# Ranking a router's experts: half-size lists packed two products to a matmul, and the fullest expert read once

## The reference, cut to what matters

```python
def moe_swiglu(x, w_router, w1, w3, w2):      # 8 experts, top 2, hidden width 3584
    ...
    logits = (xf @ w_router).astype(jnp.float32)
    top_vals, top_idx = lax.top_k(logits, TOP_K)
    gates = jax.nn.softmax(top_vals, axis=-1)
    ...
        return (jax.nn.silu(xb @ w1[e]) * (xb @ w3[e])) @ w2[e]
    ...
    out = jax.ops.segment_sum(y, tok_buf, num_segments=n)
...
        e = jax.nn.sigmoid(h @ ple_gate_w[i] + ple_gate_b[i]) * (p[i] @ ple_w[i])
        h = layer_norm(DEEPNORM_ALPHA * h + f + e, ln2_g[i], ln2_b[i])
```

## Time and profile before

| | us |
|---|---|
| device time, median of 3 runs | 2062.16 |
| lowest and highest | 2061.69, 2062.79 |
| the profiled execution: span from first to last instruction | 2060.3 |
| PE busy in that span | 2035.3 |
| DVE, ACT busy | 1579.0, 1269.3 |

### The profile page before, as it was taken

One profiled execution on the slowest core, in us unless ns is written; L12 is line 12 of the kernel. 1 busy time (PEld: TensorE's weight loads), 2 busy tenths in 40 slices (PEclk: granted clock), 3 DMA queues, 4 the chain that ended last, 5 costly groups with the idle time before them and its releaser, 6 DMA issues.

```text
span 2060.3 us, 29349 instructions
## 1 busy us (share of the span) xinstructions
PE 2035.3 (99%) x10989; PEld 1699.0 (82%) x10989; DVE 1579.0 (77%) x1430; ACT 1269.3 (62%) x1272; POOL 163.2 (8%) x134
## 2 busy tenths in 40 slices
PE   9999999999999999999999999999999999999998
PEld 8977897778889998987778888888888888888876
DVE  7767544687666557679988888888888888888897
ACT  7666433453644334466677777777777777777674
POOL 0031010000214000021400000000000000000100
PEclk9999999999999999999999999999999999999999
DMA  6533594237555555726999999999999999999995
GB/s 254 186 103 105 196 358 169 83 131 261 159 185 202 189 185 187 255 90 228 358 412 383 367 384 370 371 380 368 382 370 381 368 371 380 368 382 370 383 381 211
DMA packets 88065, 580.41 MB, mean 282 GB/s; under 512 B 10144, under 2 KB 13472, under 8 KB 22064
## 3 DMA queue, kind: packets, MB, share of 16 engines
q1 hardware_dynamic: 79472, 548.26, 70.7%
q0 software_dynamic: 7904, 29.95, 4.0%
q10 hardware_dynamic: 608, 1.07, 0.2%
HBM read 559.96 MB, written 15.73 MB: 279 GB/s over the span
## 4 chain that ended last, share of the span: by engine, by line
PE 91%; DVE 4%; DMA 1%; issue 1%; ACT 1%; POOL 0%; DVEq 0%; ACTq 0%; SPq 0%
PE bank L642 84%; PE bank L1414 1%; DMA ring<-in_w_moe 1%; DVE wrest L2634 1%; PE bank L857 1%; PE bank L1217 1%; DVE wrest L2040 0%; DMA cst<-in_consts 0%; PE bank L860 0%; PE bank L1385 0%; PE bank L1031 0%; PE bank L945 0%; PE bank L975 0%; PE bank L1224 0%; ACT ohi L1737 0%
## 5 line engine op out<-in xcount | busy, mean ns | idle before, releaser
L2634 DVE TENSOR_TENSOR wrest<-ring,whi 128x2048 fp32r<-128x2048 f32 x378 | 853.7, 2304 | 77.7 <-ACT whi L1939 77.3
L1939 ACT ACTIVATE whi<-ring 128x2048 fp32r<-128x2048 f32 x374 | 699.2, 1918 | 84.1 <-DMA ring<-in_w_moe 82.0
L642 PE MATMUL bank<-whi,xgT 128*128 128x512 f32 x1008 | 404.7, 402 | 3.0 <-DVE wrest L2634 3.0
L642 PE MATMUL bank<-wrest,xgT 128*128 128x512 f32 x1008 | 396.3, 393 | 0.0
L642 PE MATMUL bank<-whi,xgR 128*128 128x512 f32 x1008 | 393.5, 390 | 0.0
L642 PEld LDWEIGHTS bank<-whi,xgT 128*128 128x128 f32 x1008 | 189.5, 188 | 47.3 <-DVE wrest L2634 7.1
L642 PEld LDWEIGHTS bank<-whi,xgR 128*128 128x128 f32 x1008 | 189.5, 188 | 46.6
L642 PEld LDWEIGHTS bank<-wrest,xgT 128*128 128x128 f32 x1008 | 188.9, 187 | 38.7
L642 PE MATMUL bank<-whi,hidE 128*128 128x512 f32 x504 | 201.8, 400 | 0.8 <-DVE wrest L2634 0.8
L642 PE MATMUL bank<-wrest,hidE 128*128 128x512 f32 x504 | 197.8, 392 | 0.0
L642 PE MATMUL bank<-whi,hidR 128*128 128x512 f32 x504 | 196.8, 390 | 0.0
(11 more groups left out here) (483 smaller groups left out, 3688.5 us busy)
## 6 DMA issues: line engine op xcount, KB each, us to landing
ring<-in_w_moe SPq DMA_DIRECT2D x378, 1024.0 KB, 4.9
ring<-in_w_dense SPq DMA_DIRECT2D x135, 1024.0 KB, 4.8
row<-in_rows POOLq DMA_DIRECT2D x17, 512.0 KB, 5.2
xg_rows<-ncR POOLq DMA_DIRECT2D x12, 512.0 KB, 25.2
y_rows<-arena POOLq DMA_DIRECT2D x9, 512.0 KB, 6.2
arena<-xg_rows SPq DMA_DIRECT2D x9, 512.0 KB, 5.4
arena<-arena SPq DMA_DIRECT2D x32, 106.5 KB, 3.8
arena<-in_tbias POOLq DMA_DIRECT2D x2, 1536.0 KB, 8.8
```

The lines of the kernel that those rows point to most:

```text
L642: ins = pe.matmul(out_, lhsT, rhs, start=start, stop=stop, **more)
L1939: S["w_hi"].on(a.activation(whi[:, n % HI_SLOTS, :], ring[:, c % RING, :], ACT.Copy))
L2634: S["w_lo"].on(v.tensor_tensor(wrest[:, s, :], ring[:, s, :], whi[:, n % HI_SLOTS, :].bitcast(F32), ALU.subtract))
```

## The change

The experts are ranked by their counts (`rank_of`). Three kinds of list take the place of one.

- **Mid lists.** Ranks 1 and 2 (`MIDS` = 2), and one extra list for each expert that holds more than its cap, run as loops through `mid_list`, which is the old list code. The caps are 192 tokens for rank 0, 128 for ranks 1 and 2, 64 for the rest.
- **Small lists.** Ranks 3 to 7 have at most 64 tokens in them. The rounded part and the rest of the activations lie side by side in one stationary operand of 128 (`packed`), and a chunk costs two matmuls per block in place of three: 8 in all (`pair_product`). The two halves of the result's rows are added by a product with `fold_ones`, which also transposes (`fold`, eight float32 matmuls of 64 columns); ACT copies the w1 and w3 products to SBUF for it (`copy_h1`, `copy_h3`).
- **The big list.** Rank 0's weights are read once for 192 tokens: 128 by `split_product` (12 matmuls a chunk) and 64 more by `pair_product` (8), 20 in all. Its outputs are added in `y_big` by DVE, four 512-column additions a step (`add_big`).

The big list's 42 chunks and the small lists' 210 are merged in one written-out order of 252 places: a big chunk every 5.25 places up to place 215, then 36 small chunks. In this late part there are eight raw places and four rounded ones: two of `whi`'s six places become raw ones. Of the experts' weights none is loaded before the ranks are known, and two gather products stand behind the embedding gate's last chunk.

```diff
+N_SMALL, HALF = 5, P // 2
+LATE_RING, LATE_HI = 8, 4
+MIDS, EXTRAS = 2, 4
+BLOCKS = 1 + MIDS + EXTRAS + (1 + N_SMALL) // 2
...
-EMBED_AT, Y_AT = (4, 8, 12, 15, 18, 21), (20, 24, 28, 32)
+EMBED_AT, Y_AT = (4, 8, 12, 15, 18, 21), (234, 238, 242, 246)
+PAIR_LOADED, PAIR_TURNED, LAST_TURNED = (20, 112), (34, 129), 160
...
+def _merged_order():
+
+    small = []
+    for t in range(SMALL_STEPS):
+        small += [("small", t, c) for c in range(4)]
+        if t:
+            small += [("small", t - 1, c) for c in (4, 5)]
+    small += [("small", SMALL_STEPS - 1, c) for c in (4, 5)]
+    big = [("big", d, c) for d in range(E_STEPS) for c in range(6)]
+    places = {k * 21 // 4 for k in range(len(big))}
+    small, big = iter(small), iter(big)
+    return [next(big) if m in places else next(small) for m in range((1 + N_SMALL) * E_CHUNKS)]
...
+FOLD_AT = [min(m for m in range(AT["small", t, 3] + 1, LAST) if ORDER[m][0] == "small") for t in range(SMALL_STEPS)]
+BIG_FOLD_AT = [AT["big", d, 3] + 2 for d in range(E_STEPS)]
...
-            def expert(i, e):
+            def mid_list(i, e):
...
-            with sp.Fori(0, N_EXP) as e:
-                expert(e, e)
+                sp.dma_start(xg, xg_rows[bass.ds((i + 2) * P, P), :]).then_inc(x_in, 16)
...
             wait(sp, "router_done", 1)
-            n = sp.value_load(plan_i[0:1, 0:1], min_val=N_EXP, max_val=LISTS)
...
+            mid_list(0, expert_id(0))
+            wait(sp, "router_done", 3)
+            mids = sp.value_load(plan_i[0:1, ID_LISTS:ID_LISTS + 1], min_val=MIDS, max_val=MIDS + EXTRAS)
...
+            for m, (kind, step, c) in enumerate(ORDER):
+                if kind == "small" and step % E_STEPS == 0 and c == 0:
+                    small_ids[step // E_STEPS] = expert_id(ID_SMALL + step // E_STEPS)
+                e = big_id if kind == "big" else small_ids[step // E_STEPS]
+                sp.wait_ge(chunks_used.sem, mids * E_CHUNKS + (N_DENSE + (min(m - RING + 1, 0) if m < LATE_RING
+                                                                         else m - LATE_RING + 1)))
+                sp.dma_start(late_raw(m), w_moe[bass.ds(e * E_CHUNKS + in_expert(step % E_STEPS, c), 1)]
+                             .rearrange("a p n -> p (a n)")).then_inc(late_ready(m), 16)
+                if m in PAIR_LOADED:
...
+            def gather_first():
+
+                wait(pe, "places", 1)
+                gather_product(sel, (2, 3), "m_g")
+                wait(pe, "places", 2)
+                wait(pe, "pg_in", 6)
+                gather_product(selg, half_banks[0], "b_g")
...
-                        gather_first()
...
+                if i:
+                    gather_first()
...
+            def fold(bank, parts, done):
+
+                for n in range(2):
+                    for b in range(4):
+                        ins = pe.matmul(ps[bank][:, 256 * n + HALF * b:256 * n + HALF * b + HALF],
+                                        parts[n][:, b * P:(b + 1) * P], fold_ones, start=True, stop=True, skip_group_check=True)
+                S[done].on(ins)
+
...
+            def small_second(m, t, half):
+
+                l, j = divmod(t, E_STEPS)
...
+                wh, wr = late_chunk(m, 4)
+                for k in range(4):
+                    kk = 4 * (c % 2) + k
+                    split_product(ps[4 + c // 2][:, :], (big_x[0][:, kk, :], big_x[1][:, kk, :]),
+                                  (wh[:, k, :], wr[:, k, :]), kk == 0, kk == KT - 1)
...
+                for k in range(4):
+                    kk = 4 * (c % 2) + k
+                    ins = pair_product(ps[6 + c // 2][:, :], packed[:, PACKED_BIG, kk, :], (wh[:, k, :], wr[:, k, :]),
+                                       kk == 0, kk == KT - 1)
+                chunks_used.on(ins)
...
-            round_ahead(0)
-            round_ahead(1)
             wait(a, "r_top", 2)
             S["r_e"].on(a.activation(g12[:, 1, :], g12[:, 0, :], ACT.Exp))
-            round_ahead(2)
             gate_embedding(1, 0)
             round_gathered(0, 2)
+            round_ahead(0)
+            wait(a, "b_g", 1)
+            for n in range(2):
+                S["b_xa"].on(a.activation(big_x[0][:, 4 * n:4 * n + 4, :],
+                                          ps[half_banks[0][n]][:, :].rearrange("p (k n) -> p k n", k=4), ACT.Copy))
+            round_ahead(1)
+            gate_embedding(1, 1)
+            round_ahead(2)
             round_ahead(3)
-            gate_embedding(1, 1)
...
+            def copy_h1(t):
+                finished("small", t, 1)
+                wait(a, "s_fold", t)
+                S["s_copy1"].on(a.activation(s13[0], ps[0][:, :], ACT.Copy))
...
+            for m in range(AHEAD, LAST + 1):
+                wait_late(a, m, mids)
+                a.wait_ge(chunks_used.sem, mids * E_CHUNKS + (N_DENSE + m - LATE_HI + 1))
+                S["w_hi"].on(a.activation(whi[:, m % LATE_HI, :], late_raw(m), ACT.Copy))
+                if m == AHEAD:
+                    copy_outputs(mids)
+                for d in range(E_STEPS):
+                    if m == AT["big", d, 1] + 2:
+                        silu_big(d)
+                        copy_big(d, 0)
+                    if m == AT["big", d, 3] + 2:
+                        copy_big(d, 1)
...
+                for t in range(SMALL_STEPS):
+                    if m == AT["small", t, 1] + 2:
+                        copy_h1(t)
+                    if m == AT["small", t, 3] + 2:
+                        copy_h3(t)
+                    if m == FOLD_AT[t] + 2:
+                        silu_small(t)
+                    if m == min(FOLD_AT[t] + 4, LAST):
+                        round_small(t)
...
+            def add_big(d, n):
+
+                finished("big", d, 5)
+                wait(v, "b_y", 4 * d)
+                for c in range(2):
+                    part, bank = y_big[n][:, 512 * c:512 * c + 512], ps[4 + 2 * n + c][:, :]
+                    S["b_y"].on(v.tensor_tensor(part, part, bank, ALU.add) if d else v.tensor_copy(part, bank))
...
+            for m in range(AHEAD, LAST + 1):
+                wait(v, "w_hi", mids * E_CHUNKS + (MOE_ROUNDED + m + 1))
+                S["w_lo"].on(v.tensor_tensor(late_rest(m), late_raw(m), whi[:, m % LATE_HI, :].bitcast(F32), ALU.subtract))
```

More of the change, by code:

```diff
@@ L597, in _ @@
                         power(rstd[:, j:j + 1], 1)
[L600 removed]
+            wait(pool, "places", 3)
             wait(pool, "ple_done", 20)
@@ L1457, in expert_list @@
                         second(j - 1, j if j == E_STEPS - 1 else None)
-                if not last:
-                    turn_gathered(i)
+                turn_gathered(i)
                 second(E_STEPS - 1)
                 assert n[0] == E_CHUNKS and over[0] == 1
-            with pe.Fori(0, last_list) as i:
-                expert_list(i, False)
-            wait(pe, "places", 3)
-            wait(pe, "pg_in", 8)
-            for t in range(2):
-                ins = pe.transpose(ps[5][:, t * P:(t + 1) * P], selg[:, t, :], ident)
@@ L1469, in _, with late_chunk, pair_product @@
-            S["place_ps"].on(ins)
-            expert_list(last_list, True)
-            wait(pe, "places", 4)
+            with pe.Fori(0, mids) as i:
+                mid_list(i)
+            def late_chunk(m, k):
+                wait(pe, "w_lo", mids * E_CHUNKS + (MOE_RESTS + m + 1))
+                form = "p (k n) -> p k n"
+                return whi[:, m % LATE_HI, :].rearrange(form, k=k), late_rest(m).rearrange(form, k=k)
+            def pair_product(out_, both, w, start, stop):
+                mm(out_, both, w[0], start=start, stop=False, skip_group_check=True)
+                return mm(out_, both, w[1], start=False, stop=stop, skip_group_check=True)
@@ L1473, in _ @@
+            assert over[0] == 0
+            wait(pe, "b_y", 4 * E_STEPS)
             for q in range(4):
@@ new lines, in finished, with copy_h3 @@
+            def finished(kind, step, c):
+                a.wait_ge(chunks_used.sem, mids * E_CHUNKS + (N_DENSE + AT[kind, step, c] + 1))
+            def copy_h1(t):
+                finished("small", t, 1)
+                wait(a, "s_fold", t)
+                S["s_copy1"].on(a.activation(s13[0], ps[0][:, :], ACT.Copy))
+            def copy_h3(t):
+                finished("small", t, 3)
+                wait(a, "s_fold", t)
+                S["s_copy3"].on(a.activation(s13[1], ps[1][:, :], ACT.Copy))
@@ new lines, in silu_small, with round_small, copy_low @@
+            def silu_small(t):
+                wait(a, "s_fold", t + 1)
+                wait(a, "s_hid", t)
+                S["s_sl"].on(a.activation(slT, ps[1][:, 0:SEQ], ACT.Silu))
+            def round_small(t):
+                wait(a, "s_hid", t + 1)
+                if t >= 2:
+                    finished("small", t - 2, 5)
+                S["s_hi"].on(a.activation(hidP[t % 2][:, :, 0:HALF], hidT.rearrange("p (b n) -> p b n", b=4), ACT.Copy))
+            def copy_low(l):
```

(21 more changed lines are left out.)

542 lines of the change are left out of this document (436 added, 106 removed).

## The result

| | before | after |
|---|---|---|
| device time, median of 4 runs | 2062.12 us | 1981.71 us |
| lowest and highest | 2061.69, 2062.79 | 1979.84, 1982.41 |
| span of the profiled execution | 2060.3 us | 1979.3 us |

The ratio is 0.9609, with a 95% interval of 0.9595 to 0.9622: 80 us less, where the prediction had 111 less (1951, range 1895 to 2000). It is past the forecast's own narrower range, 1930 to 1975.

What follows compares the result with a forecast made beforehand. PE was taken as the bound. Mid lists ending at 1213.0 us (start's 12.7 included), late part 721 and end 14.7 gave span 1948.7; with about 1.9 for device time, 1951 us, range 1895 to 2000.

Steps and rivals of the forecast that it cites:

- The sum of the parts: Likeliest case, whole kernel: start, mid lists, late part and end added up to 1951 us; chance 0.44, own range 1930 to 1975.
- every wait costs: Rival, late part: ACT's other 85 of 133 waits cost too; 1994 us at half a us each, 2036 at one; chance 0.20.
- Lists and chunks: Expert lists: no expert over its cap, so 2 mid, 1 big and 5 small lists, 336 chunks where 378 were.
- The start: Before list 0's chunk 4: loads wait for ranks and DVE's queued work delays rests; costs 12.7 us, bounds 5.4 and 20.
- a handing over: Late part: PE's product goes through ACT's copy or silu, ACT's next rounding and DVE's rest; 4.75 us with one copy.
- The end: After the last chunk: work as before, 14.7 us.
- 30 short places ... 29 us: Late places 0 to 215: copies and silus with two small chunks and no fold behind fall short by 1.06 or 0.86 us.
- The last 36 places 90: Last 36 small chunks: PE 88 us with 11 short places, DVE 83, loads 89, so level at 90 us.
- Handing over is hidden: Rival, late part: DVE's finished stock carries PE over the short places; late part 671 us, total 1901; chance 0.20.
- Loads are the limit at 375: Rival, late part: 375 GB/s is the load ceiling and 426 a burst; total 1962 us; chance 0.10.
- One list more: Rival, mid lists: one expert over its cap adds a mid list of 120.6 us; total 2071 us; chance 0.04.
- The clock falls: Rival, late part: PE's short pauses lower its clock, 0.23 us more per affected matmul; a third of them makes 2145; chance 0.02.

Runs made afterwards that it cites:

- e5: Changed kernel with DVE's rests 2 and 3 ahead of the router's small operations and ACT's rounding of chunk 2 ahead of the embedding gate's second half: 1981.50 us.
- e10: Changed kernel with 28 small router operations and six that build selections put behind DVE's rests 4 to 16 of list 0: 1984.88 us.
- e6: Changed kernel with `packed` filled by ACT and DVE before the late part's first four roundings and rests: 1975.19 us.
- e3: Changed kernel with the first copy one rounding later, and silu and the product behind it one chunk later: 1960.90 us.
- e1: Changed kernel with only the first copy (`copy_h1`) one rounding later: 1967.61 us.
- e9: Changed kernel with the edits of e3 and e6 together: 1954.15 us.
- e7: e3 with the second copy (`copy_h3`) and the big list's silu and copy also a place later: median 1969.35 us.

## Why the prediction was right, and where it was off

**The sum of the parts** held in sign and mostly in size, though every piece but the end came out longer, so nothing was cancelled by luck, and the 1981.7 lies beyond the forecast's own range, in what the prediction gave to the lower half of "every wait costs". Lists and chunks: 336 loads. The start's DVE order and the 4.75 us of a handing over (4.78) came out as worked out. A fold is 1.78 us (1.70 and the slower first matmul behind it) against 1.7. The end is 14.5 against 14.7.

**The start**, 2.7 us over. The list of DVE's operations was right. What failed is "it ends near 979.8" for rest 4, and that PE begins chunk 4 then: rest 4 ended near 981.2, half of that for a wait for ACT that I hadn't counted, and PE wasn't ready before 982.5, since it had half the clock for chunk 2. Neither reordering of DVE's work (e5, e10) gave any of it back.

**A missing term**, about 7 us of the 17 in the first 216 places: the wait for `packed` (4.21) and 11 matmuls at 0.20 more each. I had counted what each queue issues, but not gone through the order of DVE's queue at the passage from one loop to the next, as I had at the start. e6 gives back 6.5.

**"30 short places ... 29 us"**, with 10 each for big places and catching up: mis-sized. There are 67 waits with 68 us, which count a part that PE's running matmuls still cover; 582 of PE's own work, 7 for the passage and 3 for folds leave some 56 of the 648.1 for handing over, where I had 49. So the 17 us over are these 7, the passage's 7 and the folds' 3. More places are late than the written order makes late, 67 against 37. e3 shows that I also had the cure too large: it gave 21 where all of the charge would have been 40 or more.

**"The last 36 places 90"**, 10 us over. I charged PE 77 us and 11 short places of 1 us; it waited 24 times, 25.1 us, and 100.1 less 77 is 23. I made DVE's work 83 us. It had five operations more than I counted, four weighted outputs of 1.28 and an addition of 1.21, 6 us, on the engine that was already level with PE, and PE's 3.09 us for the last hidden part and the slow matmuls behind it weren't in it either. That these make up the rest is argued: no run takes them away. Moving the handing over doesn't remove it, since e3, with both moves, still needs 96.8.

**Rivals.** *Handing over is hidden*: no, e1 to e3. *Loads are the limit at 375*: no; in the changed kernel ACT never waits for a load between 1225 and 1965 us, and where PE let it, slices 22 and 39 of the page's 40 show 406 and 425 GB/s. The Trainium skill's 358 GB/s per core ("DMA: Bandwidth & Descriptors", "Where 436 GB/s comes from") is what the late part moved on average, but not a ceiling: the same part moved 370 GB/s over 620 us in e9. *Every wait costs*: partly, and of the rivals it came nearest. PE waited 90 times from 1225 to 1965 us, 42 over the 48 that I charged, half of the other 85. The late part took 748.2 us; the sum had 721 and this rival, at half a us each, 764. But 7 of the 27 us over are the passage, which is no wait of this kind. *One list more*: no. *The clock falls*: I gave it 0.02 as an even fall, and priced it nowhere in the likeliest case. In the changed kernel's lists it fell three times, for 12, 11 and some 7 matmuls, 6 us in all.

## What to carry to other kernels

Where one engine does a piece of work that several queues hand to each other, follow the order of the slowest helper's queue at each passage between stages, not only in the steady loop: the two longest stops here, 5.85 and 4.21 us, were both PE waiting behind what stood earlier in DVE's queue. A new order gave 6.5 us for the second and nothing for the first, where DVE had no time to spare. When the time between two needs shrinks (here from 5.54 to 3.69 us), place copies and activations behind one more rounding, one kind at a time: two such moves gave 21 us, and a third took them away. And read an edit's effect on the engines that aren't in it: in e7, moves on ACT left DVE without a pause for 30 us, and POOL's gather waited.

## What the hardware showed that I had not expected

- The lower clock (1.2 of 2.4 GHz) behind short stops of PE. After 4.21, 5.85 and 6.61 us matmuls ran 0.43 us apart in place of 0.231 for about 5 us. After pauses of 2.46 us it came once (e3, 1938.03: the first matmul took 0.79) and once not (e9, 1932.44: 0.49); in the changed kernel the pauses between 1240 and 1860, mostly of 0.8 to 1.2 us and the longest of 2.23, left the clock at 1.00. The three long stops cost their length and some 2 us more.
- DVE and POOL stop each other. DVE operations of 0.17 and 0.23 us took 2.37 and 2.40 beside POOL's sums (in the kernel before, too, two rests at 969.94 took 6.11 us beside POOL's sum in place of 4.49), and POOL's indirect DMA took 12.01 and 13.54 us to issue in place of 1.85 while DVE's operations with two SBUF operands stood end to end.
